# Three pads of 32 bytes ahead of the matmul operands of a two-layer float32 kernel

## What is computed

```python
h = x                                   # (256, 2048)
hn = rmsnorm(h, mix_norm_g)
h = h + nsa_mixer(hn, ...)              # 16 heads; compressed, selected and windowed attention; @ w_out
z = rmsnorm(h, ffn_norm_g) @ ffn_w_in   # 2048 -> 2 * 5632
h = h + (silu(a) * b) @ ffn_w_out       # 5632 -> 2048
x = rmsnorm(h, final_norm_g)
proj = rmsnorm(x, norm_pre_w) @ w_in    # 2048 -> q, k, v, o, z, gates, u, z_b, g_a, g_b
y_a = mlstm(q, k, v, ...) * silu(z)     # 2048 wide
y_b = multiscale_pool(u) ... * silu(z_b)   # 1024 wide
merged = sigmoid(g_a) * (y_a @ w_proj_mlstm) + sigmoid(g_b) * (y_b @ w_proj_pool)
x = x + rmsnorm(merged @ w_out, norm_post_w)
```

## The kernel before

| tensor | begins at, before | modulo 64 | modulo 128 | modulo 64 / 128 after |
|---|---|---|---|---|
| `w_hi`, `w_lo` (each slot 4,096 bytes) | 32,896 to 61,568 | 0 | 0 | 0 / 0 |
| `x_hi`, `x_lo` | 65,664 and 82,048 | 0 | 0 | 32 / 32 |
| `h` | 98,432 | 0 | 0 | 0 / 64 |
| `f_hi`, `f_lo` | 128,608 and 173,664 | 32 | 96 | 32 / 32 |
| `ya_hi`, `ya_lo` | 128,608 and 144,992 | 32 | 96 | 32 / 32 |
| `yb_hi`, `yb_lo` | 161,376 and 169,568 | 32 | 96 | 32 / 32 |
| `m_hi`, `m_lo` | 177,760 and 194,144 | 32 | 96 | 32 / 32 |
| `o_hi`, `o_lo` | 179,072 and 195,456 | 0 | 0 | 32 / 96 |
| `prob`, `prob_t`, `prob_ct`, `bias_g` (behind `o_lo`) | 211,840 and on | 0 | 0 | 32 / 96 |
| `pm_t` (second layer) | 224,672 | 32 | 32 | 32 / 96 |

## Time and profile before

### The profile page before, as it was taken

One profiled execution on the slowest core, in us unless ns is written; L12 is line 12 of the kernel. 1 busy time (PEld: TensorE's weight loads), 2 busy tenths in 40 slices (PEclk: granted clock), 3 DMA queues, 4 the chain that ended last, 5 costly groups with the idle time before them and its releaser, 6 DMA issues.

```text
span 2272.6 us, 44428 instructions
## 1 busy us (share of the span) xinstructions
PE 2225.1 (98%) x17654; PEld 2179.0 (96%) x17654; DVE 1346.2 (59%) x1562; ACT 955.8 (42%) x1190; POOL 176.4 (8%) x215
## 2 busy tenths in 40 slices
PE   8999999999999999999999999999999999999996
PEld 7989999999999999999999999999999999999996
DVE  7656554665555555545566676755766665455475
ACT  4444555344343444333344354343443443334442
POOL 5000322200000000001222000000000000000022
PEclk9999999999999999999999999999999999999998
DMA  6557333455555555555555455555545455555553
GB/s 234 180 187 242 122 121 108 160 181 185 182 180 183 173 190 181 184 186 168 175 180 172 158 178 175 179 170 171 187 159 176 167 178 182 187 185 183 182 181 102
DMA packets 111590, 396.11 MB, mean 174 GB/s; under 512 B 12178, under 2 KB 16290, under 8 KB 111472
## 3 DMA queue, kind: packets, MB, share of 16 engines
q1 hardware_dynamic: 109344, 386.97, 51.8%
q0 software_dynamic: 2128, 7.38, 1.0%
HBM read 389.83 MB, written 2.13 MB: 172 GB/s over the span
## 4 chain that ended last, share of the span: by engine, by line
PE 93%; DVE 4%; ACT 1%; issue 1%; DMA 1%; POOL 0%; SPq 0%; ACTq 0%; DVEq 0%
PE set L1272 27%; PE set L1274 26%; PE set L1273 26%; PE set L1286 3%; PE set L1288 3%; PE set L1287 3%; DVE x_lo L758 1%; DVE w_lo L739 1%; DMA raw<-in_weights 1%; PE misc L1435 1%; PE misc L1421 1%; ACT w_hi L503 1%; PE misc L1576 0%; PE misc L1437 0%; PE misc L1436 0%
## 5 line engine op out<-in xcount | busy, mean ns | idle before, releaser
L739 DVE TENSOR_TENSOR w_lo<-raw,w_hi 128x1024 fp32r<-128x1024 f32 x730 | 907.6, 1252 | 766.9 <-ACT w_hi L503 762.4
L503 ACT ACTIVATE w_hi<-raw 128x1024 fp32r<-128x1024 f32 x730 | 766.2, 1056 | 1036.5 <-PE set L1274 941.3
L1272 PE MATMUL set<-x_hi,w_hi 128*128 128x256 f32 x3584 | 1027.1, 287 | 10.2 <-DVE w_lo L739 7.8
L1273 PE MATMUL set<-x_lo,w_hi 128*128 128x256 f32 x3584 | 1017.1, 284 | 0.0
L1274 PE MATMUL set<-x_hi,w_lo 128*128 128x256 f32 x3584 | 1016.8, 284 | 0.0
L1272 PEld LDWEIGHTS set<-x_hi,w_hi 128*128 128x128 f32 x3584 | 690.9, 193 | 14.0 <-DVE w_lo L739 8.6
L1273 PEld LDWEIGHTS set<-x_lo,w_hi 128*128 128x128 f32 x3584 | 691.1, 193 | 1.0
L1274 PEld LDWEIGHTS set<-x_hi,w_lo 128*128 128x128 f32 x3584 | 690.8, 193 | 0.0
L1272 PE MATMUL set<-f_hi,w_hi 128*128 128x256 f32 x704 | 199.6, 284 | 6.4 <-DVE w_lo L739 4.0
L1273 PE MATMUL set<-f_lo,w_hi 128*128 128x256 f32 x704 | 199.2, 283 | 0.0
L1274 PE MATMUL set<-f_hi,w_lo 128*128 128x256 f32 x704 | 199.1, 283 | 0.0
(11 more groups left out here) (282 smaller groups left out, 2451.9 us busy)
## 6 DMA issues: line engine op xcount, KB each, us to landing
raw<-in_weights SPq DMA_DIRECT2D x730, 512.0 KB, 3.6
bias_g<-bias POOLq DMA_DIRECT2D x4, 572.0 KB, 3.8
cur<-in_cur POOLq DMA_DIRECT2D x4, 535.0 KB, 3.7
h<-in_x SPq DMA_DIRECT2D x4, 512.0 KB, 8.3
bias<-u_dram POOLq DMA_DIRECT2D x1, 2048.0 KB, 14.2
out<-y_t SPq DMA_DIRECT2D x4, 512.0 KB, 3.3
w<-in_w POOLq DMA_DIRECT2D x1, 256.0 KB, 6.8
vm<-in_causal POOLq DMA_DIRECT2D x1, 192.0 KB, 4.7
```

Source lines behind the costliest of these rows:

```text
L503: a(w_hi[at.slot(j)][:, :], raw[at.slot(j)][:, :], ACT.Copy).then_inc(hi_ready, 1)
L739: tt(w_lo[s][:, :], raw[s][:, :], w_hi[s][:, :].bitcast(F32), ALU.subtract).then_inc(lo_ready, 1)
L1272: mm(o, w_hi[slot][:, c:c + P], hi[:, kt, :], start=starts, stop=False, skip_group_check=True)
L1273: mm(o, w_hi[slot][:, c:c + P], lo[:, kt, :], start=False, stop=False, skip_group_check=True)
```

## The change

Three tensors of 8 float32 values (32 bytes per partition) are declared that nothing reads or writes: one ahead of `x_hi`, one behind `x_lo`, one ahead of `o_hi`. No instruction is added, removed or put elsewhere in the order. `x_hi` and `x_lo` begin 32 bytes later, everything behind them 64 bytes later, and from `o_hi` to the end of its scope 96 bytes later. Nineteen empty lines at the head of the file go too, so line numbers fall by 19 and later by less.

```diff
-
...
     w_hi = [sb(f"w_hi{n}", [P, CC], F32R) for n in range(RING)]
     w_lo = [sb(f"w_lo{n}", [P, CC], F32R) for n in range(RING)]
+
+    sb("pad0", [P, 8])
     x_hi = sb("x_hi", [P, KT, S], F32R)
     x_lo = sb("x_lo", [P, KT, S], F32R)
+    sb("pad1", [P, 8])
     h = sb("h", [P, KT, S])
...
         with ExitStack() as s1c:
+            sb("pad2", [P, 8], scope=s1c)
             o_hi = sb("o_hi", [P, HEADS, S], F32R, scope=s1c)
             o_lo = sb("o_lo", [P, HEADS, S], F32R, scope=s1c)
```

## The result

The changed kernel takes 2240.88 us (median of 4, 2233.67 to 2243.84) against 2271.51 us for the kernel before (median of 4, 2267.88 to 2273.37). The ratio is 0.9862, 95% interval 0.9843 to 0.988: 31 us faster, where 19.6 were forecast. The way was right, the size was not.

A forecast was written before the change was run, and what follows sets the result against it. The prediction took TensorE's matmul count times pitch as the bound. Gains of 17.6 (x), 1.2 (o) and 0.8 us (tokens form) sum to 19.6, taking the median from 2270.4 to 2250.8, said as 2251 us; range 2246 to 2260.

The forecast's parts named there:

- What bounds the kernel, and that the pitch moves it: Whole kernel: TensorE busy 2225.1 of 2272.6 us, so time is nearly the number of matmuls times the pitch of each.
- The two kinds of stream: TensorE's matmul streams: x and o at about 120.0 ns a matmul, f and ya at 118.3, told apart by tensor start.
- What the slow kind shares: Streams of x and o: tensors begin at a multiple of 64 bytes; all fast ones begin 32 bytes behind one.
- The term of x: Lines 1272 to 1274, x_hi and x_lo moving: 10,650 matmuls gain 1.65 ns each, 17.6 us.
- What moves with them: Other shifted tensors, prob, prob_t, bias_g and VectorE's operands, including the mixed read at line 758: all costed at 0.
- the rival of a 128-byte period: Moving operands: only 96 modulo 128 is fast, so x stays, o gains, others lose; net +5.4 us, 2275.8; chance 0.08.
- o, 1.2 us: o_hi and o_lo as moving operands: 752 matmuls gain 1.65 ns each, 1.2 us.
- The tokens form, a gain of 0.8 us: Weights move, x stationary, 960 matmuls: 0.8 us gain taken, between 1.6 us gain and 0; loss bounded at 1.6 us.
- The range: Median time of the changed kernel: 2246 to 2260 us, holding the forecast and the half gain, leaving out the other two.
- long enough that the starts of this one execution hardly matter: Reason given for the forecast's chance of 0.79: streams this long make one execution's starts nearly irrelevant.
- no effect: Rival: the shift does nothing and the two kinds of stream have a missed cause; 2270.4 us, chance 0.07.
- half of it comes back: Rival: x gains, but line 758 stalls, lower-clock stretches, late chunks or a stationary-operand loss take part; 2260 us, chance 0.06.

The follow-up runs named there:

- The run at +8: Against the changed kernel, weight slots become slices of one tensor and pads put all activation operands 8 bytes past the weights: 2246.1 us (one run).

## Why the prediction was right in its way and wrong in its size

- *What bounds the kernel, and that the pitch moves it:* right. Of the 34 us, 4.5 are a shorter time at the lower clock, and 29.6 are left for the pitches; there is nothing in the end behind the streams, and the waits stayed.
- *The two kinds of stream are due to where the operands lie:* right, and shown by undoing x alone.
- *"What the slow kind shares is that the tensor begins at a multiple of 64 bytes, as its weights do":* wrong as a rule. Moved along with the weights, a multiple of 64 is good and 32 behind one is bad. The half sentence on the weights was the true part.
- *The term of x, 10,650 by 1.65 ns = 17.6 us:* this is the step that failed, by size. The 118.3 ns were f's and ya's, at -32 from the weights; x went to +32. No row showed +32, and I priced it as -32. It is 116.7 or 117.8 ns, so 2.2 to 3.3 ns a matmul, 23 to 35 us. x alone brought 27 us with the loss of the tokens form (below) in it, so 31 without. x put at -32 did have 118.4 ns, and 2256 us with that loss, near the 2251 forecast; but f, ya, yb, m and o had other distances there as well.
- *"What moves with them", at 0:* f, ya, yb and m went from -32 to +32 too. I had seen that in the rival of a 128-byte period, but counted it only as a possible loss; they brought 3 us together.
- *o, 1.2 us:* 768 by 0.2 ns, nothing. It came to 352 and not to +32.
- *The tokens form, a gain of 0.8 us:* a loss of 6.4 ns at 576 matmuls, 3.7 us, beyond the bound of 1.6 that I had put on it. I took the size of the gain for that of the possible loss without a row. The 384 narrow ones changed little: a mean duration of 287 ns, where the earlier trace rows have 290.
- *The range:* 2246 to 2260 stood on pitches between 118.3 and 120.0. A place without a row should have been bounded on the side of a gain too, by the columns alone (106.7 ns) at the far end. The spread of the runs, 10 us in the changed kernel, wasn't foreseen either: "long enough that the starts of this one execution hardly matter" was wrong, as the third stretch of f shows.
- *The rivals:* the period of 128 and no effect fell. Of "half of it comes back" one part came true, the loss in the tokens form, and was larger than its price; the waits and the lower clock gave nothing back.

## What to carry to other kernels

Where TensorE is the bound and stationary and moving tiles come from SBUF by turns, look at the pitch of each stream and at the spread of durations: a stream that stands still at one value above the others is worth a pad. Try several distances between the two operands, since the gain here was 0 to 6.7 ns of 120 by distance and not in order of it, and take several executions and profiles of each, since one placement can have several pitches. Look at every form of product: the one that moves the weights lost here with most of the pads. Price a placement that no row shows by both ends, and list everything that a pad moves.

## What was not expected of the hardware

- The pitch of a 256-column matmul with its 128-column LDWEIGHTS, at 2.4 GHz, took values of 113.3, 116.7, 117.3 to 117.8, 118.3, 118.7 and 120.0 ns, steady for hundreds of us, depending on the distance of the two operands in bytes and differing between executions of one kernel. The Trainium skill, "SBUF — State Buffer", section "Who interferes with whom", calls TensorE's two read ports, for the moving operand and for LDWEIGHTS, independent. In these runs the two operands are not independent of each other: moving both by 32 bytes changes nothing (2273.9 us), moving one against the other gave 2229.0 to 2280.2 us. Whether they meet at the ports or behind them no run shows.
- The lines of 16 bytes in the Trainium skill, "SBUF — State Buffer", section "Door 1: The DMA port swizzle", don't tell the placements apart. With x alone at +16 both operands begin on multiples of 16, as before, and the pitch is 113.3 ns instead of 120.0. The run at +8 is no test inside one line, as its expectation has it: the weights begin 8 bytes behind a multiple of 16 there and the activations on the next multiple.
- The 512-column tokens form had 226.9 ns at distance 0 and 233 to 234 at +32, +64, +96 and -32 with the weights on a multiple of 32: the same shift helps one form and hurts the other. At +16 the stretch from 117 to 160 us had 233.3 ns in one execution and about 226.5 in another of the same kernel.
- Open is what in the chip produces the patterns, what picks one of them, and why a start off a multiple of 32 changes them. The patterns are shown, a cause below them isn't.
